# Encoder trunk, head pairs: which of a level half's two side works is issued first

## The chip, the cores and the metric

One NeuronCore of a Trainium2 chip runs the whole program. The metric is the device time of one execution, in microseconds, as the median of several runs.

## The reference

A streaming encoder step with two layers. Each layer mixes tokens through two branches that share one input projection, and then runs an MLP. Tokens are 512 of a prompt and 8 x 16 of running streams, 640 in all; the model width is 1024.

```
z = h @ w_in                                  # one projection for all branches
r, k, v, zw, zi, zg = split(za_mix)           # RWKV-7 branch, 16 heads of 64
S = S * w + (S a) b^T + v k^T ;  y = S r      # per frame, per head
y = group_norm(y) + (sum(r * k * a_rk)) * v ; y = y * gate
# retention branch: 4 heads, chunked; both merged by sigmoid gates, then w_out, then the MLP
```

The kernel computes the recurrence S in blocks of 128 tokens. Inside a block that needs the inverse of a triangular matrix, which is built in levels, each doubling the size of the inverted blocks.

## The kernel before

The 16 heads are worked through in 8 pairs a layer, `rwkv(l, p)`. A pair has five token blocks and two heads, so ten small problems. They are treated in three groups of four, four and two. After products of the blocks (points t, z) come levels 1 to 6. Each level has two halves. In the **T half** TensorE multiplies for each group (marks T), and VectorE multiplies the result by a mask into `T1`. In the **X half** TensorE multiplies T1 (marks X), and ScalarE evicts the result to `XX` or `XTF`. The T half of a level waits for the evictions of the level before it, the X half for the masks. After the levels come a long product (uw) and a chain over the blocks (ca, cb).

Between these dependent pieces the kernel puts independent work of two kinds:

- **Quarters.** While a pair runs, ten tiles of the layer's input projection are made, each in four quarters of 12 matmuls (128x320, with `h_hi`, `h_lo`, `w_hi`, `w_lo`). `point("la3")` issues as many quarters as the table `POINTS` says: two in every half of a level. So a tile starts at each lb and ends at the next la. All tiles use the same two PSUM banks: a tile's first quarter waits until ScalarE has evicted the tile before (L1246, or L1239 for the tiles r, k, v of the next pair). On ScalarE, `point` evicts the tile behind its last quarter, with Copy, Silu or Sigmoid, and then makes the high part `w_hi` of the next weight tile (the high split, L1142). On VectorE, `point` makes its low part `w_lo` (the low split, L1545).
- **Steps of the neighbours.** `side` is a Python generator, one per engine, that first does the group norm of pair p-1 and then prepares pair p+1. `next(side, None)` issues its code up to the next `yield`. All engines call it equally often, so a step stands at the same place on all of them. TensorE's steps, by the name that each marks, lie so: rows behind X1, over behind X2, gate behind X3, wi0 behind T4, wi1 behind X4, ss behind T5, kb behind T6, bs behind X6. The other steps of the levels are empty on TensorE. ss sums squares over channels (128x2 matmuls); ScalarE takes the square root (`KR`, 128x10), VectorE the reciprocal (L1698), and kb spreads it over the channels. wi0 and wi1 feed sigmoids on ScalarE, which then squares k for ss.

Each engine runs its own instructions in the order in which they are written; semaphores (`wait_stage`, `done`) tie the engines together. ScalarE loads a new function table where the next function needs one; the compiler places this instruction. In the levels, pairs 1 and 6 evict a Silu tile in level 4, and pairs 1, 4 and 6 one in level 5; the others evict with Copy there, and pair 7, which prepares nothing, with Sigmoid.

Of the kernel before, what the change touches and what calls it, by code (L numbers as in the profile page):

```python
# [151 lines left out]
def rw_groups(lv):  # L152

    return (0, 1, 2) if lv < S_LEVELS else (0, 1)


def group_blocks(g):

    return range(4 * g, min(4 * g + 4, 2 * NBLK))
# [67 lines left out]
def build(nc, io, outs, scratch):  # L227
# [8 lines left out]
    with ExitStack() as ctx:  # L236
# [388 lines left out]
        def _(pe):  # L625
# [179 lines left out]
            def rwkv(l, p):  # L805
# [3 lines left out]
                point, side = quarters_of(l, f"f{p}"), beside_of(l, p)  # L809
# [42 lines left out]
                for lv in range(1, LEVELS):  # L852
                    for g in rw_groups(lv):
                        if lv == 1:
                            W("ve_in", f"x0.{g}")
                        else:
                            W("ac_in", f"X{lv - 1}.{g}")
                        for m in group_blocks(g):
                            to = slice(64 * (m % 4), 64 * (m % 4) + 64)
                            if lv == LEVELS - 1:  # L860
                                last = mm(ps[64:128, 2 + g, to], LTI[0:64, m, 64:128], XX[0:64, m, 0:64])
                                continue
                            for d in range(2):
                                last = mm(ps[half(d), 2 + g, to], LTI[half(d), m, half(d)], XX[half(d), m, 0:64])
                        M(last, "pe_in", f"T{lv}.{g}")
                    point(f"la{lv}")
                    next(side, None)
                    for g in rw_groups(lv):
                        W("ve_in", f"T{lv}.{g}")
                        for m in group_blocks(g):  # L870
                            at_ = 128 * (m % 4)
                            if lv == LEVELS - 1:
                                last = mm(ps[0:64, 2 + g, 64 * (m % 4):64 * (m % 4) + 64], T1[64:128, m], XTF[64:128, m, 64:128])
                                continue
                            ends = g == 2 and lv == S_LEVELS - 1
                            for d in range(0 if ends else 1 if lv == LEVELS - 2 else 2):
                                mm(ps[half(d), 2 + g, at_:at_ + 64], XX[half(d), m, 64:128], T1[half(d), m])
                            for d in range(2):
                                last = mm(ps[half(d), 2 + g, at_ + 64:at_ + 128], T1[half(d), m], XX[half(d), m, 64:128])
                        M(last, "pe_in", f"X{lv}.{g}")  # L880
                    point(f"lb{lv}")
                    next(side, None)
                W("ac_in", "z")
                W("ac_in", f"X{S_LEVELS - 1}.2")
                for g in (0, 1):
# [237 lines left out]
        def _(ac):  # L1123
# [192 lines left out]
            def rwkv(l, p):  # L1316
                n = PAIRS * l + p
                W = lambda stage, name: wait_stage(ac, stage, n, name)
                M = lambda stage, name: done(stage, n, name)
                point, side = evictions_of(l, f"f{p}"), beside_of(l, p)  # L1320
                for b in range(NBLK):
                    W("pe_tr", f"t{b}")
                    do(TOKB[:, 4 * b:4 * b + 4], ps[:, 6 + b % 2, :].rearrange("p (t n) -> p t n", n=128))
                    M("ac_tr", f"t{b}")
                    point(f"t{b}" if b < PB else "z")
                W("pe_in", "z")
                do(Z_.rearrange("p m n -> p (m n)"), five_blocks(5))
                M("ac_in", "z")
                point("z")
                next(side, None)  # L1330
                point("lt")
                next(side, None)
                for lv in range(1, LEVELS):
                    point(f"la{lv}")
                    next(side, None)
                    for g in rw_groups(lv):
                        W("pe_in", f"X{lv}.{g}")
                        ms = slice(4 * g, 2 * NBLK if g == 2 else 4 * g + 4)
                        k = 2 if g == 2 else 4
                        src = ps[:, 2 + g, 0:128 * k].rearrange("p (t n) -> p t n", n=128)  # L1340
                        if lv == LEVELS - 1:
                            do(XTF[0:64, ms, 64:128], ps[0:64, 2 + g, 0:64 * k].rearrange("p (t n) -> p t n", n=64))
                        elif lv == LEVELS - 2 or g == 2 and lv == S_LEVELS - 1:
                            if g != 2:
                                do(XX[0:64, ms, 0:64], src[0:64, :, 0:64])
                            for d in range(2):
                                do(XTF[half(d), ms, half(d)], src[half(d), :, 64:128])
                        else:
                            do(XX[:, ms], src)
                        M("ac_in", f"X{lv}.{g}")  # L1350
                    point(f"lb{lv}")
                    next(side, None)
                W("pe_in", "uw")
                by_stream = lambda a: a.rearrange("p (m b t) -> p m b t", m=2, t=DEC_T)
                do(WT, ps[:, 4, :].rearrange("p (t n) -> p t n", n=128))
                do(WRS[:, :, :, 0:DEC_T], by_stream(ps[:, 7, 0:128]))
                do(WRS[:, :, :, DEC_T:2 * DEC_T], by_stream(RR[:, p % 2, SEQ:TOK]))
                M("ac_in", "uw")
                point("uw")
                next(side, None)  # L1360
                for c in range(PB):
                    point(f"ca{c}")
                    next(side, None)
                    if c == 0:
                        W("pe_ch", "sT")
                        for e in range(2):
                            do(STS[:, 2 * e:2 * e + 2], ps[:, 5 + e, 0:256].rearrange("p (m e v) -> p m e v", e=2, v=64))
                        M("ac_ch", "sT")
                    if c == 1:
                        W("pe_ch", "su")  # L1370
                        do(SU.rearrange("p (b t) -> p b t", t=DEC_T), ps[:, 6, 0:256].rearrange("p (b n) -> p b n", n=2 * DEC_T)[:, :, 0:DEC_T])
                        M("ac_ch", "su")
                    if c == 3:
                        W("pe_ch", "y")
                        if p:
                            wait_stage(ac, "ve_gn", n - 1, "ya")
                            ac.wait_ge(ya_lo, PAIRS * l + min(p, 4))
                        do(yb[:, 0:SEQ], ps[:, 7, :])
                        do(yb[:, SEQ:TOK].rearrange("p (b t) -> p b t", t=DEC_T), ps[:, 6, 0:256].rearrange("p (b n) -> p b n", n=2 * DEC_T)[:, :, DEC_T:2 * DEC_T])
                        M("ac_ch", "y")  # L1380
                    point(f"cb{c}")
                    next(side, None)
                for _ in side:
                    pass
                W("pe_ch", "spo")
                if n:
                    ac.wait_ge(rw_out, 96 * n)
                do(SPO[0:64, :], ps[0:64, 4, 0:128])
                M("ac_ch", "spo")
                W("pe_ch", "sout")  # L1390
                do(SN, ps[:, 2, :].rearrange("p (b n) -> p b n", n=128))
                M("ac_ch", "sout")
                point("end")
# [129 lines left out]
        def _(ve):  # L1523
# [254 lines left out]
            def rwkv(l, p):  # L1778
# [3 lines left out]
                point, side = low_parts_of(l, f"f{p}"), beside_of(l, p)  # L1782
# [25 lines left out]
                for lv in range(1, LEVELS):  # L1808
                    for g in rw_groups(lv):
                        W("pe_in", f"T{lv}.{g}")  # L1810
                        k = 2 if g == 2 else 4
                        src = ps[:, 2 + g, 0:64 * k].rearrange("p (t n) -> p t n", n=64)
                        if lv == LEVELS - 1:
                            after(ve.tensor_copy(T1[64:128, 4 * g:4 * g + k], src[64:128]))
                        else:
                            c = C_LC + 64 + 64 * lv
                            tt(T1[:, 4 * g:4 * g + k], src, c1[:, None, c:c + 64].to_broadcast([128, k, 64]), MUL_)
                        M("ve_in", f"T{lv}.{g}")
                    point(f"la{lv}")
                    next(side, None)  # L1820
                    point(f"lb{lv}")
                    next(side, None)
                point("uw")
                next(side, None)
                parity = c1[:, None, C_EP:C_EP + 2, None].to_broadcast([128, 2, 2, 64])
# [212 lines left out]
```

## Time and profile before

| | us |
|---|---|
| median of 3 runs | 5024.22 (5024.21 to 5031.55) |
| the profiled execution's own time | 5024.12 |
| its span, first to last instruction | 5022.3 |
| TensorE busy | 4492.5 |
| VectorE busy | 2025.7 |
| ScalarE busy | 1378.9 |

Busy time is that in which an engine executes at least one instruction. A stretch in which one engine is nearly always busy runs at that engine's pace; what others do there costs nothing unless it makes the busy one wait. In a timeline row the numbers are the start and the length in us, and a bracket tells how long the engine stood idle before the row, and for whom. A matmul in f32 appears as two records, so five matmuls read x10. L634 is the helper through which nearly all matmuls go; L1129 is ScalarE's.

### The profile page before, as it was taken

Reading aid. Unit: us, or ns where it says so; the run is one execution under the profiler, and the core shown is the slowest. Engines: PE = TensorE matmul, PEld = TensorE weight load, DVE = VectorE, ACT = ScalarE, POOL = GpSimd, SP = SyncE. Lnnn points to the kernel's source line nnn. Section 1 sums busy time; section 2 is a strip of 40 time slices with the busy share of each in tenths; the row PEclk is TensorE's granted clock in tenths of the full one; section 3 lists DMA queues with packets and bytes.
Section 4 is the critical chain, followed back from the end, with each engine's and each line's share of the span. In section 5 each row is a group of like instructions: output and inputs, shape, how many; then the busy total and the mean of one; then the engine's idle time right before and its main releaser. Section 6 shows DMA issues by size and latency. Waiting matters only on the chain.

```text
span 5022.3 us, 87846 instructions
## 1 busy us (share of the span) xinstructions
PE 4492.5 (89%) x38284; PEld 3916.8 (78%) x38284; DVE 2025.7 (40%) x2870; ACT 1378.9 (27%) x1995; POOL 237.3 (5%) x393
## 2 busy tenths in 40 slices
PE   6899999999987777899978999999999777779997
PEld 1689889888865557899917888888888565569996
DVE  0434444434234444544415444444433444354444
ACT  1333333333211112322303333333332111122222
POOL 0000000000010001000000000000000100100000
PEclk9899999999999988999988999999999999989998
DMA  7211122112343324122261211112124433412221
GB/s 246 65 62 59 59 64 61 60 60 67 127 134 131 132 95 126 44 74 83 61 231 44 64 60 57 60 61 64 59 70 131 156 126 124 128 56 70 71 74 60
DMA packets 481278, 448.78 MB, mean 89 GB/s; under 512 B 17638, under 2 KB 399472, under 8 KB 480000
## 3 DMA queue, kind: packets, MB, share of 16 engines
q1 hardware_dynamic: 432624, 291.02, 18.7%
q0 software_dynamic: 30896, 119.06, 7.2%
q10 hardware_dynamic: 17408, 33.56, 1.7%
q8 instruction: 278, 4.55, 0.4%
q14 instruction: 72, 0.59, 0.0%
HBM read 345.81 MB, written 97.76 MB: 88 GB/s over the span
## 4 chain that ended last, share of the span: by engine, by line
PE 81%; DVE 7%; DMA 7%; ACT 4%; issue 2%; ACTq 0%; DVEq 0%; SPq 0%; POOL 0%; POOLq 0%
PE ps L634 79%; ACT scr L1129 2%; DVE scr L1532 2%; DMA scr<-in_ada_w_dram 2%; PE ps L638 2%; DMA scr<-in_state_ret_dram 2%; DMA out_dram<-scr 1%; DMA w_raw<-in_w_branch_b_dram 1%; DVE scr L1534 1%; ACT w_hi L1142 1%; DVE scr L1610 1%; DVE scr L1919 1%; DVE w_lo L1545 1%; DVE acc L1532 1%; DMA w_raw<-in_w_in_dram 0%
## 5 line engine op out<-in xcount | busy, mean ns | idle before, releaser
L634 PE MATMUL ps<-scr 64*64 64x64 f32 (+10 forms) x15136 | 1164.4, 259 | 133.6 <-DMA scr<-in_state_ret_dram 60.5
L634 PEld LDWEIGHTS ps<-scr 64*64 64x64 f32 (+5 forms) x15136 | 820.8, 146 | 503.2 <-issue 351.5
L634 PE MATMUL ps<-h_hi,w_hi 128*128 128x320 f32 x4288 | 1033.5, 323 | 107.3 <-DVEq L1540 76.8
L634 PE MATMUL ps<-h_lo,w_hi 128*128 128x320 f32 x4288 | 984.5, 311 | 0.0
L634 PE MATMUL ps<-h_hi,w_lo 128*128 128x320 f32 x4288 | 983.0, 311 | 0.0
L634 PEld LDWEIGHTS ps<-h_hi,w_hi 128*128 128x128 f32 x4288 | 707.3, 190 | 161.0 <-issue 126.6
L634 PEld LDWEIGHTS ps<-h_lo,w_hi 128*128 128x128 f32 x4288 | 724.1, 190 | 0.0
L634 PEld LDWEIGHTS ps<-h_hi,w_lo 128*128 128x128 f32 x4288 | 723.9, 190 | 0.0
L1129 ACT ACTIVATE scr<-ps 128x512 f32<-128x512 f32 (+9 forms) x694 | 346.3, 499 | 1344.5 <-PE ps L634 1100.8
L1142 ACT ACTIVATE w_hi<-w_raw 128x1024 fp32r<-128x1024 f32 (+1 forms) x468 | 410.9, 878 | 782.8 <-PE ps L634 681.6
L1545 DVE TENSOR_TENSOR w_lo<-w_raw,w_hi 128x1024 fp32r<-128x1024 f32 (+1 forms) x468 | 469.0, 1002 | 352.6 <-ACT w_hi L1142 339.7
L634 PE MATMUL ps<-r_hi,w_hi 128*128 128x320 f32 x1664 | 391.8, 317 | 137.5 <-DVEq L1540 110.3
L634 PEld LDWEIGHTS ps<-r_hi,w_hi 128*128 128x128 f32 x1664 | 284.6, 193 | 147.4 <-issue 144.6
L634 PE MATMUL ps<-r_lo,w_hi 128*128 128x320 f32 x1664 | 386.9, 314 | 0.0
L634 PE MATMUL ps<-r_hi,w_lo 128*128 128x320 f32 x1664 | 386.2, 314 | 0.0
L1532 DVE TENSOR_TENSOR scr<-ps,c 128x512 f32<-128x512 f32 (+2 forms) x416 | 221.3, 532 | 408.1 <-PE ps L634 372.6
L634 PEld LDWEIGHTS ps<-r_lo,w_hi 128*128 128x128 f32 x1664 | 285.5, 193 | 0.0
L634 PEld LDWEIGHTS ps<-r_hi,w_lo 128*128 128x128 f32 x1664 | 285.2, 192 | 0.0
L1532 DVE TENSOR_TENSOR scr<-scr 128x640 f32<-128x640 f32 (+6 forms) x292 | 263.9, 904 | 15.2 <-ACTq L1228 2.2
L634 PE MATMUL ps<-scr,c 64*64 64x64 f32 (+1 forms) x1024 | 167.4, 316 | 53.7 <-ACTq L1135 51.3
L1534 DVE SCALAR_TENSOR_TENSOR scr<-scr,ps 128x1024 f32<-128x1024 f32 x64 | 78.1, 1221 | 301.9 <-PE ps L634 301.9
L1246 ACT ACTIVATE scr<-ps 128x640 f32<-128x640 f32 x128 | 90.1, 704 | 379.6 <-PE ps L634 379.0
(131 smaller groups left out, 2860.9 us busy)
## 6 DMA issues: line engine op xcount, KB each, us to landing
w_raw<-in_w_in_dram SPq DMA_DIRECT2D x180, 512.0 KB, 3.7
scr<-in_ada_w_dram SPq DMA_DIRECT2D x24, 2048.0 KB, 7.9
scratch_z<-scr SPq DMA_DIRECT2D x128, 320.0 KB, 2.2
scr<-in_state_ret_dram POOLq DMA_DIRECT2D x64, 512.0 KB, 5.3
out_dram<-scr ACTq DMA_DIRECT2D x64, 512.0 KB, 3.4
w_raw<-in_w_ffn_up_dram SPq DMA_DIRECT2D x64, 512.0 KB, 4.0
w_raw<-in_w_ffn_down_dram SPq DMA_DIRECT2D x128, 256.0 KB, 2.8
scr<-scratch_z POOLq DMA_DIRECT2D x8, 2560.0 KB, 9.8
```

Source lines behind the costliest of these rows:

```text
L634: return pe.matmul(out, lhsT, rhs, start=start, stop=stop, skip_group_check=True)
L638: return pe.transpose(out, in_, c1[0:n, C_ID:C_ID + n])
L1129: ac.activation(out, in_, f, **kw).then_inc(ac_order, 1)
L1142: ac.activation(WH[:, s, 0:kt], WR[:, s, 0:kt], ACT.Copy).then_inc(hi_done, 1)
L1246: ac.activation(halves(ZT[:, f % 2]), two_banks(0), fn).then_inc(psum_read_a, 1)
L1532: tt = lambda o, a, b, op: after(ve.tensor_tensor(o, a, b, op))
L1534: stt = lambda o, a, s, b, o0, o1: after(ve.scalar_tensor_tensor(o, a, s, b, o0, o1))
L1545: ve.tensor_tensor(WL[:, s, 0:kt], WR[:, s, 0:kt], WH[:, s, 0:kt].bitcast(F32), SUB).then_inc(lo_done, 1)
L1610: after(ve.reciprocal(RS, RS))
L1919: after(ve.reciprocal(PT[:, 0:TOK], PT[:, 0:TOK]))
```

## The change

In every level half, on TensorE, ScalarE and VectorE, the side step is called ahead of `point` and not behind it. All else stays.

```diff
--- before.py
+++ after.py
@@ -863,8 +863,8 @@
                             for d in range(2):
                                 last = mm(ps[half(d), 2 + g, to], LTI[half(d), m, half(d)], XX[half(d), m, 0:64])
                         M(last, "pe_in", f"T{lv}.{g}")
+                    next(side, None)
                     point(f"la{lv}")
-                    next(side, None)
                     for g in rw_groups(lv):
                         W("ve_in", f"T{lv}.{g}")
                         for m in group_blocks(g):
@@ -878,8 +878,8 @@
                             for d in range(2):
                                 last = mm(ps[half(d), 2 + g, at_ + 64:at_ + 128], T1[half(d), m], XX[half(d), m, 64:128])
                         M(last, "pe_in", f"X{lv}.{g}")
+                    next(side, None)
                     point(f"lb{lv}")
-                    next(side, None)
                 W("ac_in", "z")
                 W("ac_in", f"X{S_LEVELS - 1}.2")
                 for g in (0, 1):
@@ -1331,8 +1331,8 @@
                 point("lt")
                 next(side, None)
                 for lv in range(1, LEVELS):
+                    next(side, None)
                     point(f"la{lv}")
-                    next(side, None)
                     for g in rw_groups(lv):
                         W("pe_in", f"X{lv}.{g}")
                         ms = slice(4 * g, 2 * NBLK if g == 2 else 4 * g + 4)
@@ -1348,8 +1348,8 @@
                         else:
                             do(XX[:, ms], src)
                         M("ac_in", f"X{lv}.{g}")
+                    next(side, None)
                     point(f"lb{lv}")
-                    next(side, None)
                 W("pe_in", "uw")
                 by_stream = lambda a: a.rearrange("p (m b t) -> p m b t", m=2, t=DEC_T)
                 do(WT, ps[:, 4, :].rearrange("p (t n) -> p t n", n=128))
@@ -1816,10 +1816,10 @@
                             c = C_LC + 64 + 64 * lv
                             tt(T1[:, 4 * g:4 * g + k], src, c1[:, None, c:c + 64].to_broadcast([128, k, 64]), MUL_)
                         M("ve_in", f"T{lv}.{g}")
+                    next(side, None)
                     point(f"la{lv}")
                     next(side, None)
                     point(f"lb{lv}")
-                    next(side, None)
                 point("uw")
                 next(side, None)
                 parity = c1[:, None, C_EP:C_EP + 2, None].to_broadcast([128, 2, 2, 64])
```

On TensorE a place in level 5 of pair 0: `scr 64x64 x16` is the T5 product, `c,scr 128x2 x5` the step ss, and `h_..,w_..` are quarters. Before:

```order
L634 MATMUL ps<-h_lo,w_hi 128x320 x2
L634 MATMUL ps<-h_hi,w_lo 128x320 x2
L634 MATMUL ps<-c,scr 128x2 x5
L634 MATMUL ps<-scr 64x64 x24
L634 MATMUL ps<-h_hi,w_hi 128x320 x2
```

and now:

```order
L634 MATMUL ps<-scr 64x64 x16
L634 MATMUL ps<-c,scr 128x2 x5
L634 MATMUL ps<-h_hi,w_hi 128x320 x2
L634 MATMUL ps<-h_lo,w_hi 128x320 x2
L634 MATMUL ps<-h_hi,w_lo 128x320 x2
```

ss stood behind the two quarters and in front of X5; it now stands behind T5 and in front of the quarters.

On ScalarE level 4 of pair 1: L1246 evicts the tile, `r_hi` is the group norm's last step, `ps,par 128x320 x2` are the sigmoids behind wi0 and wi1, `128x4x128 x2` the evictions of X4, `acc,par` the square for ss.

```order
-L1246 ACT_TABLE_LOAD
-L1246 ACTIVATE scr<-ps 128x640
-L1142 ACTIVATE w_hi<-w_raw 128x1024
 L1129 ACTIVATE r_hi<-scr 128x640
 L1129 ACT_TABLE_LOAD
 L1129 ACTIVATE scr<-ps,par 128x320 x2
-L1129 ACTIVATE scr<-ps 128x4x128 x2
+L1246 ACT_TABLE_LOAD
+L1246 ACTIVATE scr<-ps 128x640
+L1142 ACTIVATE w_hi<-w_raw 128x1024
+L1129 ACTIVATE scr<-ps 128x4x128 x2
+L1129 ACT_TABLE_LOAD
```

The tile's eviction and the high split went behind the step, and one table load more stands between the two pairs of sigmoids.

On VectorE from the reciprocal of level 5 to the multiply behind kb in level 6 of pair 0 (`w_lo` is a low split, L1814 the mask step of T6, `scr<-scr,ps` the multiply):

```order
 L1698 RECIPROCAL scr<-scr 128x10
+L1545 TENSOR_TENSOR w_lo<-w_raw,w_hi 128x1024
 L1814 COPY scr<-ps 64x256 x2
 L1533 TENSOR_SCALAR scr<-scr,par 128x640
 L1534 SCALAR_TENSOR_TENSOR acc<-scr,acc 128x640
 L1534 SCALAR_TENSOR_TENSOR scr<-acc,par 128x640
-L1545 TENSOR_TENSOR w_lo<-w_raw,w_hi 128x1024
 L1532 TENSOR_TENSOR scr<-scr,ps 128x640
```

The low splits moved behind the step: one from ahead of the reciprocal to behind it, one from ahead of the multiply to behind it.

## Rows read from the trace of the kernel before

**Rows 1.** The page: the span and its first part, busy time by engine.

```profile
span 5022.3 us, 87846 instructions
...
PE 4492.5 (89%) x38284; PEld 3916.8 (78%) x38284; DVE 2025.7 (40%) x2870; ACT 1378.9 (27%) x1995; POOL 237.3 (5%) x393
```

**Rows 2.** Busy time (instructions) in two stretches: pairs of layer 0, of layer 1.

```profile
260.00:1320.00 1060.00, 1046.80 (x12137) 941.60 (x12137) 432.27 (x759) 357.14 (x566) 42.42 (x70) 1.00 0.20 62
2750.00:3830.00 1080.00, 1066.44 (x12311) 959.72 (x12311) 438.81 (x767) 363.33 (x577) 46.05 (x76) 1.00 0.20 63
```

**Rows 3.** The chain of waits of TensorE, stretch 260 to 1320.

```profile
PE ps L634 <- ACT scr L1246: 9.3, 12, 1.7
PE ps L634 <- ACTq L1228: 3.9, 7, 1.6
```

**Rows 4.** Timeline of TensorE (start, us), pair 1 of layer 0, levels 4 to 6.

```profile
437.78 0.56 PE L634 MATMUL ps<-h_hi,w_hi 128*128 128x320 f32 x2
...
441.50 0.81 PE L634 MATMUL ps<-scr,lw 64*128 64x320 f32 x4
442.24 2.08 PE L634 MATMUL ps<-scr 64*64 64x64 f32 x64
...
448.70 1.22 PE L634 MATMUL ps<-scr 64*64 64x64 f32 x32
449.85 0.56 PE L634 MATMUL ps<-h_hi,w_hi 128*128 128x320 f32 x2
...
453.47 1.17 PE L634 MATMUL ps<-c,scr 128*128 128x2 f32 x10
454.57 2.08 PE L634 MATMUL ps<-scr 64*64 64x64 f32 x48
456.58 0.56 PE L634 MATMUL ps<-h_hi,w_hi 128*128 128x320 f32 x2
...
460.29 1.14 PE L634 MATMUL ps<-scr 64*64 64x64 f32 x16
461.36 0.55 PE L634 MATMUL ps<-h_hi,w_hi 128*128 128x320 f32 x2
...
465.07 1.31 PE L634 MATMUL ps<-c,scr 128*64 128x128 f32 x20
```

**Rows 5.** Timeline of ScalarE in the same pair and levels.

```profile
441.65 1.28 ACT L1246 ACT_TABLE_LOAD   x1 [8.33 <-PE ps L634]
...
447.82 1.31 ACT L1129 ACTIVATE scr<-ps 128x512 f32<-128x512 f32 x2
449.26 1.09 ACT L1129 ACTIVATE scr<-ps,par 128x320 f32<-128x320 f32 x2
450.74 0.83 ACT L1129 ACTIVATE scr<-acc,par 128x640 f32<-128x640 f32 x1 [0.40 <-DVEq L1663]
453.72 1.28 ACT L1246 ACT_TABLE_LOAD   x1 [2.15 <-PE ps L634]
455.01 0.70 ACT L1246 ACTIVATE scr<-ps 128x640 f32<-128x640 f32 x1
...
456.56 2.51 ACT L1129 ACTIVATE scr<-ps 64x256 f32<-64x256 f32 x6
...
460.47 0.18 ACT L1129 ACTIVATE scr<-ps 128x10 f32<-128x10 f32 x1
```

**Rows 6.** Timeline of VectorE in the same pair, levels 5 and 6.

```profile
460.80 0.17 DVE L1533 TENSOR_SCALAR scr<-scr 128x10 f32<-128x10 f32 x1 [1.22 <-ACTq L1228]
461.01 0.22 DVE L1698 RECIPROCAL scr<-scr 128x10 f32<-128x10 f32 x1
...
463.97 0.89 DVE L1534 SCALAR_TENSOR_TENSOR scr<-acc,par 128x640 f32<-128x640 f32 x1
```

**Rows 7.** Timeline of TensorE behind the last pair, where a step precedes quarters.

```profile
1338.05 1.17 PE L634 MATMUL ps<-c,scr 128*128 128x2 f32 x10
1339.08 0.54 PE L634 MATMUL ps<-h_hi,w_hi 128*128 128x320 f32 x2
```

## Prediction, written before the changed kernel ran

> **What bounds the kernel now.** I read the page first: TensorE (PE) is busy for 4492.5 of 5022.3 us, the next engine, VectorE, for 2025.7 [rows 1]. The change touches only the stage of the head pairs, so I asked for the busy time of that stage in both layers. There PE is busy for 1046.80 of 1060.00 us and for 1066.44 of 1080.00 us, at the full granted clock of 1.00, which is 2.4 GHz [rows 2]: 13.2 and 13.6 us of idle time are all that better cover could win. The chain of waits says what they are in layer 0: 9.3 us in 12 waits for a tile's eviction (L1246) and 3.9 us in 7 waits at a pair's start [rows 3]. By their place in the timeline these lie at the points uw, ca and cb and at the pair's first transposes; none lies in a level, which is where the change is. So the stage goes at the pace of PE's own instructions, and an edit matters if it makes PE wait or changes what it costs to go from one kind of matmul to the next.
>
> **What moves.** In each of six levels a T half and an X half both had: products of the level, two quarters (24 matmuls), the side step. Now the step stands ahead of the quarters. Nothing is added on PE, VectorE, SyncE or GpSimd. DMA issues keep their order; SyncE's loads wait for the low splits, which VectorE now does up to one step later. On ScalarE two table loads a layer are added, in pairs 1 and 6, where the tile evicted in level 4 is a Silu tile and now comes between two uses of Sigmoid.
>
> A pair's active PE steps in the levels are rows, over, gate (pairs 1 to 7) and wi0, wi1, ss, kb, bs (pairs 0 to 6): 3 x 14 + 5 x 14 = 112 moved steps. Each used to have two quarters, 3.71 us (456.58 to 460.29 in [rows 4]), in front of it as cover for what it waits for. That cover now stands behind it. For each I ask what its input's chain takes.
>
> **Terms that come to nothing.** rows needs a VectorE and a ScalarE instruction behind the T masks, over a small sqrt with its table load, gate one multiply: each chain is under 4 us, against the T half's quarters and the X products (3.71 + 2.01 us) that still lie between. wi0 and wi1 wait for work a half level older. bs waits for kb's multiply on VectorE: from the reciprocal at 461.01 to the end of three more operations (463.97 + 0.89) takes 3.9 us [rows 6]; with a low split (about 1.1) now in between and the multiply (0.8) behind, some 6.0 us, against 0.4 + 1.24 + 3.71 + 1.07 = 6.4 us until PE is at bs. It fits by 0.4 us. The low splits that come later feed a tile that starts a level (11 us) on.
>
> **The term kb (level 6).** kb waits for the reciprocal of the root of ss. That chain runs over ScalarE, which serves in this order: eviction of level 5's tile, high split, six evictions of X5, table load, sqrt; then VectorE's max and reciprocal. Its start is tied to the end of the T5 quarters, and these now come later, since ss is ahead of them. Count from the end of T5, E. PE: ss to quarters 1.03 (1338.05 to 1339.08 in [rows 7]), quarters to X5 3.71, X5 2.01 (454.57 to 456.58), quarters 3.71, T6 1.07 (460.29 to 461.36) [rows 4]: PE is at kb at E + 11.53. The chain: the eviction starts 3.87 us behind its quarters' start (449.85 to 453.72), and the reciprocal ends 6.22 us behind the eviction (455.01 to 461.23) [rows 4 to 6]; a release takes 0.15 us (460.65 to 460.80). Ready at E + 1.03 + 3.87 + 6.22 + 0.15 = E + 11.27. It fits, by 0.26 us.
>
> Where the level-5 tile is Silu, a table load stands ahead of its eviction (453.72 to 455.01, 1.29 us): ready at E + 12.56, and PE **waits 1.03 us**. Before, it hid: kb came only at 465.07. These are pairs 1, 4 and 6: 3 x 1.03 = 3.1 us a layer. X5's quarters then also wait some 0.3 us for that eviction, but within the same 1.03.
>
> **The term ss (level 5), pairs 1 and 6.** With both table loads of level 4: wi0 at 437.78, its quarters at 438.52 (wi0 0.74), load at +3.87 = 442.39, eviction 443.68, behind it and the split (1.55) X4's evictions 445.23, 1.44 us on the added load 446.67, the two sigmoids 447.96, the square 449.16, done 449.99, released 450.14 [rows 4, 5]. PE is at ss at 438.52 + 3.71 + 2.01 + 0.74 + 3.71 + 1.07 = 449.76. It **waits 0.4 us**: 0.8 a layer.
>
> A load costs 1.28 us and the next activation starts 0.01 us later [rows 5]. The Trainium skill (ScalarE: Activation LUTs, What ACT_TABLE_LOAD costs) adds a drain of about 1.38 us to each switch. By that rule the wait at ss would be 1.8 us, and the sum 5.5 us higher; by the row, 0.4.
>
> **Borders between kinds of matmul.** For ss: before, T5 to quarters 1.07, quarters to ss 3.62 (449.85 to 453.47), ss to X5 1.10 (453.47 to 454.57), in all 5.79. Now T5 to ss, which no row shows (I take 1.07 to 1.15), 1.03 and 3.71: 5.81 to 5.89. I take +0.05 for each of 28 such steps (rows and ss), 1.4 us, and zero for the others, whose parts (0.74, 3.71) are the same on either side. Bounds from the nearest rows: 0.1 us either way for 112 steps, 11 us.
>
> **Sum.** 2 x (3.1 + 0.8) + 1.4 = 9.2 us on the profiled execution's own 5024.12 us, 5033.3; the median of the runs shown, 5024.22, is 0.1 above that one. **I predict 5033 us.** About 0.2%, 10 us, is what a measurement can tell from no change, so this stands at the border.
>
> **Rivals.**
> A, all hidden: 5024 to 5028. If the ScalarE chain gets shorter than I add up, or borders give back 0.05 us a step (-5.6 us). For it: work that has nothing to do moves ahead; against it, the chain of 6.22 us has no idle gap to lose. 0.20.
> B, the plain pairs wait too. The margin of 0.26 us in pairs 0, 2, 3, 5 is within what a few semaphores take; 0.3 us more in the chain costs all 14 steps 0.3: 4 us, 5037. 0.18.
> C, a border costs more: the step's first load behind 64x64 products takes 0.1 to 0.2 us longer than the quarters' did. 112 steps: 11 to 22 us, 5044 to 5055. It decides from 0.1 us on. The Trainium skill (TensorEngine Tiling (Array Packing), Key Properties) states that a change of tiling mode drains TensorE; but the changes of mode are here as many as before, only between other neighbours. 0.08.
> D, a table switch costs 2.66 us at ss, as the page has it: 5038 to 5039. The rows speak against it. 0.05.
> E, faster: early steps let ScalarE and VectorE run ahead, so that the waits of 13.2 + 13.6 us at uw, ca, cb shrink. More than 19 of these 27 must go for it to show against my 9 us: 5007 to 5014. Against it: these waits are for an eviction just behind its own quarters, which move with them. 0.04.
> My own case, 5029 to 5037, has 0.45.
>
> **Numbers.** Within 0.2% (to 5034.2): two thirds or more of my case (0.32), A (0.20) and a little of B (0.03), 0.55. Slower: the rest of mine 0.13, of B 0.15, C 0.08, D 0.05, 0.41. Faster 0.04. Of both signs little is left for the one below; the range 5026 to 5041 leaves out C, E and the low end of A.
>
> **What would show it.** Right: new waits of PE of about 1 us ahead of kb in pairs 1, 4, 6 alone, for VectorE's reciprocal, and 0.4 us ahead of ss in 1 and 6; ScalarE with four more table loads; ss to kb 11.5 us in plain pairs. Wrong: waits at kb in every pair (B), none (A), more time between the same instructions with no wait named (C), fewer waits at ca and uw (E). It fails most easily by the margins of 0.26 and 0.4 us, which are sums of five durations.

## The result, and the profile after

The changed kernel takes 5034.51 us (median of 20 runs, 5028.68 to 5040.04), the kernel before 5024.22 us over 20 runs. The ratio is 1.002, with a 95% interval of 1.0013 to 1.0027: slower by 10.3 us, or 6.5 to 13.6 us by the interval. Forecast were 5033 us and a range of 5026 to 5041; the time lies right at the border between "no change" and "slower" that the prediction drew, and a little beyond it.

The page, first the span and busy time by engine, as in [rows 1]:

```profile
span 5038.2 us, 87850 instructions
PE 4508.3 (89%) x38284; PEld 3925.9 (78%) x38284; DVE 2027.1 (40%) x2870; ACT 1379.0 (27%) x1999; POOL 237.4 (5%) x393
```

PE executes the same 38284 matmuls; ScalarE has 1999 instructions and not 1995, the four added table loads. PE's busy time rose by 15.8 us, most of it outside the changed part (see the last section).

The waits of PE in the stretch of layer 0's pairs (260 to 1325 us), as in [rows 3] (releaser, then us in total, times, longest):

```profile
PE ps L634 <- ACT scr L1246: 10.0, 15, 1.7
PE ps L634 <- ACTq L1228: 4.6, 9, 1.6
PE ps L634 <- DVEq L1663: 1.9, 3, 0.6
```

Three kinds came: three waits for VectorE (L1663 is its semaphore increment in the steps), two more for ScalarE's steps, three more for evictions. Where they are, the timeline of PE shows; pair 1 of layer 0, to be held against [rows 4] (start, length, then idle before the row):

```profile
447.72 1.15 PE L634 MATMUL ps<-scr 64*64 64x64 f32 x32
449.08 1.28 PE L634 MATMUL ps<-c,scr 128*128 128x2 f32 x10 [0.22 <-ACTq L1228]
450.22 0.54 PE L634 MATMUL ps<-h_hi,w_hi 128*128 128x320 f32 x2
...
453.91 2.08 PE L634 MATMUL ps<-scr 64*64 64x64 f32 x48
456.21 0.53 PE L634 MATMUL ps<-h_hi,w_hi 128*128 128x320 f32 x2 [0.22 <-ACT scr L1246]
...
459.89 1.14 PE L634 MATMUL ps<-scr 64*64 64x64 f32 x16
461.67 1.31 PE L634 MATMUL ps<-c,scr 128*64 128x128 f32 x20 [0.64 <-DVEq L1663]
```

ss waits 0.22 us, the quarters behind X5 wait 0.22, kb waits 0.64. ScalarE and VectorE in the same pair, against [rows 5, 6]:

```profile
454.07 1.28 ACT L1246 ACT_TABLE_LOAD   x1 [5.08 <-PE ps L634]
455.36 0.70 ACT L1246 ACTIVATE scr<-ps 128x640 f32<-128x640 f32 x1
455.96 1.05 ACT L1142 ACTIVATE w_hi<-w_raw 128x1024 fp32r<-128x1024 f32 x1
456.91 2.50 ACT L1129 ACTIVATE scr<-ps 64x256 f32<-64x256 f32 x6
459.51 1.28 ACT L1129 ACT_TABLE_LOAD   x1
460.80 0.18 ACT L1129 ACTIVATE scr<-ps 128x10 f32<-128x10 f32 x1
```

```profile
461.14 0.17 DVE L1533 TENSOR_SCALAR scr<-scr 128x10 f32<-128x10 f32 x1 [4.91 <-ACTq L1228]
461.35 0.22 DVE L1698 RECIPROCAL scr<-scr 128x10 f32<-128x10 f32 x1
```

The chain from the load to the reciprocal's end is 454.07 to 461.57, 7.50 us, and it has no gap over 0.2 us: it is as long as before (453.72 to 461.23, 7.51). What moved are its start and PE. Counted from the end of T5 in a plain pair, one without a Silu tile (pair 2 of layer 0), PE is at kb after 11.62 us (585.78 to 597.40) where it took 15.22 (585.35 to 600.57), and the quarters that start the chain begin 1.14 us later.

**Level time** is what the rest of this text compares: from the first of a pair's lt products to its first uw product, read from the starts in PE's timeline. It holds all six levels and nothing else. In the table it is given for the pairs of layer 1, where no stretch at half clock fell into a pair's levels, save with ScalarE's old order (see there and at the end); layer 0 agrees within 0.07 us a pair but for such stretches.

| level time, us, layer 1 | pair 0 | 1 | 2 | 3 | 4 | 5 | 6 | 7 | more than before, both layers |
|---|---|---|---|---|---|---|---|---|---|
| before | 71.31 | 75.88 | 75.81 | 75.82 | 75.82 | 75.82 | 75.81 | 71.01 | |
| changed | 71.42 | 77.31 | 76.04 | 76.04 | 77.09 | 76.09 | 77.67 | 71.12 | 11.0 |
| ss back | 71.31 | 75.93 | 75.94 | 75.94 | 76.01 | 75.94 | 76.01 | 71.12 | 1.9 |
| kb back | 71.42 | 77.14 | 76.04 | 76.04 | 76.85 | 76.04 | 77.44 | 71.12 | 9.6 |
| kb alone | 71.31 | 75.88 | 75.82 | 75.82 | 76.98 | 75.82 | 76.97 | 71.01 | 4.8 |
| kb and bs | 71.31 | 75.90 | 75.83 | 75.83 | 75.90 | 75.83 | 75.90 | 71.01 | 0.5 |
| levels 1 to 3 alone | 71.31 | 75.98 | 75.92 | 75.93 | 75.92 | 75.92 | 75.92 | 71.12 | 1.4 |
| ScalarE's old order | 75.23 | 84.07 | 81.80 | 81.81 | 84.10 | 79.61 | 83.44 | 72.45 | 90 |
| no Silu, old order | 71.30 | 75.81 | 75.81 | 75.82 | 75.81 | 75.82 | 75.81 | 71.01 | |
| no Silu, new order | 71.43 | 76.04 | 76.04 | 76.04 | 76.04 | 76.08 | 76.05 | 71.12 | 3.2 (than the row above) |

The last column sums the differences over 16 pairs, less 1.5 us where a stretch at half clock fell into pair 6 of layer 0 (changed, kb back). The changed kernel's 11.0 us accounts for the whole measured loss of 10.3 us, within its interval of 6.5 to 13.6.

### The profile page after: what moved, and what is told of

The parts are those of the page before. It is cut to its first block, busy times and chain, and to the rows that moved or that the text cites. A ratio compares the mean times of both kernels' runs of the same rounds, so it can differ in the third digit from the quotient of the medians.

```text
span 5038.2 us, 87850 instructions
## 1 busy us (share of the span) xinstructions
PE 4508.3 (89%) x38284; PEld 3925.9 (78%) x38284; DVE 2027.1 (40%) x2870; ACT 1379.0 (27%) x1999; POOL 237.4 (5%) x393
## 4 chain that ended last, share of the span: by engine, by line
PE 80%; DVE 7%; DMA 6%; ACT 4%; issue 2%; ACTq 0%; DVEq 0%; SPq 0%; POOL 0%; POOLq 0%
PE ps L634 78%; ACT scr L1129 3%; DVE scr L1532 2%; DMA scr<-in_ada_w_dram 2%; PE ps L638 2%; DMA scr<-in_state_ret_dram 2%; DMA out_dram<-scr 1%; DMA w_raw<-in_w_branch_b_dram 1%; DVE scr L1534 1%; ACT w_hi L1142 1%; DVE scr L1610 1%; DVE scr L1919 1%; DVE w_lo L1545 1%; DVE acc L1532 1%; ACT scr L1246 0%
## 5 line engine op out<-in xcount | busy, mean ns | idle before, releaser
L634 PE MATMUL ps<-scr 64*64 64x64 f32 (+10 forms) x15136 | 1165.6, 259 | 129.2 <-DMA scr<-in_state_ret_dram 57.1
L634 PEld LDWEIGHTS ps<-scr 64*64 64x64 f32 (+5 forms) x15136 | 822.1, 146 | 490.6 <-issue 349.4
L634 PE MATMUL ps<-h_hi,w_hi 128*128 128x320 f32 x4288 | 1034.5, 323 | 108.7 <-DVEq L1540 77.1
L634 PE MATMUL ps<-h_lo,w_hi 128*128 128x320 f32 x4288 | 982.7, 311 | 0.0
L634 PE MATMUL ps<-h_hi,w_lo 128*128 128x320 f32 x4288 | 981.6, 310 | 0.0
L634 PEld LDWEIGHTS ps<-h_hi,w_hi 128*128 128x128 f32 x4288 | 708.2, 189 | 177.3 <-issue 147.3
L634 PEld LDWEIGHTS ps<-h_lo,w_hi 128*128 128x128 f32 x4288 | 722.6, 189 | 0.0
L634 PEld LDWEIGHTS ps<-h_hi,w_lo 128*128 128x128 f32 x4288 | 722.2, 189 | 0.0
L1129 ACT ACTIVATE scr<-ps 128x512 f32<-128x512 f32 (+9 forms) x694 | 345.0, 497 | 1320.5 <-PE ps L634 1082.6
L634 PE MATMUL ps<-r_hi,w_hi 128*128 128x320 f32 x1664 | 393.2, 318 | 134.8 <-DVEq L1540 110.3
L634 PEld LDWEIGHTS ps<-r_hi,w_hi 128*128 128x128 f32 x1664 | 285.5, 194 | 144.8 <-issue 142.0
L634 PE MATMUL ps<-r_lo,w_hi 128*128 128x320 f32 x1664 | 387.7, 315 | 0.0
L634 PE MATMUL ps<-r_hi,w_lo 128*128 128x320 f32 x1664 | 387.0, 314 | 0.0
L634 PEld LDWEIGHTS ps<-r_lo,w_hi 128*128 128x128 f32 x1664 | 286.8, 193 | 0.0
L634 PEld LDWEIGHTS ps<-r_hi,w_lo 128*128 128x128 f32 x1664 | 285.9, 193 | 0.0
L634 PE MATMUL ps<-scr,c 64*64 64x64 f32 (+1 forms) x1024 | 177.1, 330 | 50.8 <-ACTq L1135 50.4
L1129 ACT ACTIVATE scr<-scr 128x640 f32<-128x640 f32 (+6 forms) x182 | 119.6, 657 | 316.3 <-DVEq L1663 195.8
```

Of the source, the lines that this page charges most:

```text
L634: return pe.matmul(out, lhsT, rhs, start=start, stop=stop, skip_group_check=True)
L1129: ac.activation(out, in_, f, **kw).then_inc(ac_order, 1)
```

## The experiments

The first edits use a helper in place of the two lines, so that each level half of each engine can be chosen. It moves the lines of the kernel: L634, L1129, L1246, L1228 and L1663 are L647, L1140, L1257, L1239 and L1672 there.

```diff
+def half_of(eng, name, point, side):
+    if name in STEP_FIRST[eng]:
+        next(side, None)
+        point(name)
+    else:
+        point(name)
+        next(side, None)
```

**1. ss back.** `STEP_FIRST` holds all halves but la5.

> As the changed kernel, but in the T half of level 5 (the step ss) the quarters stand ahead of the step again, on all three engines. Level time below is the time from the lt products to the product uw in the trace of a pair (before: 75.82 us in pairs 2 to 5). Theory (chain tied to the T5 quarters): with ss behind them these quarters start 1.03 us earlier, so the reciprocal is ready at E + 11.53 us and TensorE is at kb at E + 11.51: no wait above 0.1 us is left at kb or ss, pairs 1, 4 and 6 take as long as the plain ones, each about 0.2 us above before, and the kernel takes 5027 us. Rival 1 (kb's own loss of cover is enough): the waits of 0.64 us at kb stay in pairs 1, 4, 6 and the time is about 5032. Rival 2 (the cost is in the borders): one step of eight less, 5033 to 5034.

Measured: 5026.27 us (11 runs), ratio to before 1.0001 (0.9991 to 1.001). In layer 0's pairs PE's waits are those of the kernel before, row by row:

```profile
PE ps L647 <- ACT scr L1257: 9.3, 12, 1.7
PE ps L647 <- ACTq L1239: 3.9, 7, 1.6
```

Every new wait is gone, with kb's quarters still behind it. So it was not enough that kb lost its cover: the chain that feeds it had to start late as well. In pair 1 the chain is again 7.50 us long (453.85 to 461.35) and ends 0.14 us ahead of kb at 461.49. Where PE waits for the reciprocal, kb starts 0.1 us behind its end (461.57 to 461.67 in the changed kernel), so less than 0.05 us is to spare, as the first theory had it. 0.12 us of borders a plain pair is left.

**2. kb back.** All halves but la6.

> As the changed kernel, but in the T half of level 6 (the step kb) the quarters stand ahead of the step again. Theory: kb has its 3.7 us of cover again and never waits; what is left are the waits of 0.2 to 0.5 us at ss in pairs 1 and 6 and the wait of 0.2 us for the eviction of level 5 in pairs 1, 4 and 6, so pair 4's level time is 0.4 us above before, pair 1's 0.6, pair 6's 0.9, the plain ones' 0.2: 5029 us. Rival 1 (ss's place is what costs, kb only shows it): hardly a gain on the changed kernel, 5033. Rival 2 (borders): 5033 to 5034.

Measured: 5032.3 us (11 runs), ratio 1.0005 (0.9996 to 1.0014), level times 9.6 us above before. This is a miss: pairs 4, 1 and 6 are 1.03, 1.26 and 1.63 us above before, not 0.4, 0.6 and 0.9, and of 1.43 us in pair 1 only 0.17 went. The level times decide here, since the interval of the totals holds both no change and most of the loss. Rival 1 had forecast this (hardly a gain), but not the place of the wait. kb does not wait, but bs does, a step further on (PE, pair 1):

```profile
464.85 1.31 PE L647 MATMUL ps<-c,scr 128*64 128x128 f32 x20
466.09 1.14 PE L647 MATMUL ps<-scr 64*64 64x64 f32 x16
467.70 1.34 PE L647 MATMUL ps<-scr,c 128*128 128x320 f32 x4 [0.47 <-DVEq L1672]
```

and VectorE at that place:

```profile
461.52 0.22 DVE L1707 RECIPROCAL scr<-scr 128x10 f32<-128x10 f32 x1
461.88 1.23 DVE L1554 TENSOR_TENSOR w_lo<-w_raw,w_hi 128x1024 fp32r<-128x1024 f32 x1
463.14 1.00 DVE L1823 COPY scr<-ps 64x256 f32<-64x256 f32 x2
464.29 0.56 DVE L1542 TENSOR_SCALAR scr<-scr,par 128x640 f32<-128x640 f32 x1
464.88 0.83 DVE L1543 SCALAR_TENSOR_TENSOR acc<-scr,acc 128x640 f32<-128x640 f32 x1
465.74 0.89 DVE L1543 SCALAR_TENSOR_TENSOR scr<-acc,par 128x640 f32<-128x640 f32 x1
466.77 0.82 DVE L1541 TENSOR_TENSOR scr<-scr,ps 128x640 f32<-128x640 f32 x1
```

From the reciprocal's end at 461.74 VectorE works without a gap over 0.2 us until it can release bs at 467.70, 5.96 us. This is the chain that the prediction had put at 6.0 us and found to fit by 0.4 us. In the changed kernel's pairs 1, 4 and 6 it fits because PE has just waited at kb. Take that wait away, and it comes back at bs.

**3. kb alone.** `STEP_FIRST` is {la6}.

> As the kernel before, with only the T half of level 6 (the step kb) changed. Theory: the quarters of T5 still start 1.03 us earlier than in the changed kernel, so kb's input is ready at E + 11.53 us in the pairs with a Silu tile, against E + 11.51 for TensorE: a wait of 0 to 0.1 us, level times within 0.15 us of before, 5024 us. Rival (kb alone loses its cover): waits of about 1 us at kb in pairs 1, 4 and 6, 5030 us.

Measured: a single run, 5030.29 us. No wait at kb, as the theory had it, though by as little as in experiment 1 (the reciprocal ends 0.14 us ahead of kb in pairs 1, 4 and 6), and pairs 1, 2, 3, 5 are as before. But pairs 4 and 6 take 1.2 us more, which neither theory foresaw. PE in pair 4 of layer 0:

```profile
875.84 1.14 PE L647 MATMUL ps<-scr 64*64 64x64 f32 x16
878.14 0.53 PE L647 MATMUL ps<-h_hi,w_hi 128*128 128x320 f32 x2 [1.16 <-ACT scr L1257]
```

ScalarE:

```profile
876.00 1.28 ACT L1257 ACT_TABLE_LOAD   x1 [5.83 <-PE ps L647]
877.29 0.70 ACT L1257 ACTIVATE scr<-ps 128x640 f32<-128x640 f32 x1
```

All tiles use one pair of PSUM banks. In pairs 4 and 6 the level-6 tile is Silu, so its eviction needs 2.0 us behind the load's start. Before, kb and X6 lay between the tile's last quarter and the next tile's first; with kb moved ahead X6's 1.07 us are left, and PE waits for the bank. The step was cover for the eviction. The explanation was put to the test:

**4. kb and bs.** `STEP_FIRST` is {la6, lb6}.

> As the kernel before, with both halves of level 6 changed (steps kb and bs). In the run with kb alone, pairs 4 and 6 waited 1.16 us for the eviction of the level-6 tile, which is Silu there: TensorE had only X6 (1.07 us) between the tile's last quarter and the next tile's first. Theory: bs, moved ahead of that first quarter, gives 0.9 to 1.1 us back, so the wait is at most 0.3 us and the level times of pairs 4 and 6 fall from 77.0 to 76.1 us. Rival (the wait is for something else that kb's move delays, for instance ScalarE's order): it stays at 1.1 us.

Measured: a single run, 5026.68 us; pairs 4 and 6 at 75.90 us, 0.08 above before and 1.1 below the run with kb alone. Shown for level 6: what the la half loses as cover for the bank, the lb half gives back by its own step.

**5. ScalarE's old order.** PE and VectorE as in the changed kernel, `STEP_FIRST["ac"]` empty.

> As the changed kernel, but ScalarE keeps its old order (a tile's eviction and high split ahead of the step) in all level halves. Theory (a step is only as early as the engine that feeds it): wi1 on TensorE now comes at 5.7 us behind the start of the T4 quarters, while ScalarE gets to wi0's sigmoids behind eviction, split, in pairs 1 to 4 the group norm's conversion, and the table load, ready at 7.9 to 8.8 us, 1.3 later with a Silu tile: waits at wi1 of 2.2 us in pairs 0 and 5, 3.1 in 2 to 4, 4.4 in 1, 3.5 in 6; over waits 1.1 us in pairs 1 to 7. In all about 60 us, 5086. Rival (the idle ScalarE has slack everywhere): no more than the changed kernel, 5034.

Measured: 5116.75 us (4 runs), ratio 1.0176 (1.016 to 1.0191). The waits in layer 0's pairs:

```profile
PE ps L647 <- ACTq L1239: 24.9, 14, 4.2
PE ps L647 <- ACT scr L1257: 10.0, 15, 1.7
PE ps L647 <- DVEq L1672: 9.9, 10, 1.2
```

At wi1 they are 2.24 us in pairs 0 and 5, 2.94 in 2 to 4, 4.22 in 1 and 3.52 in 6, at over 1.13 to 1.20: the sizes expected, within 0.2 us, and 58 us in all. The engine that feeds a step has to serve it as early as PE wants it. The sum was too low by a third (60 us against 90). Most of the rest is clock: 12 stretches at half clock fell into the levels, two of them twice as long as the others, and at 1.5 us for each of the short ones (see the end) that is some 21 us, an estimate. Waits at kb and at X5's quarters, which I had left out, are 5 us, the borders 3. In the windows view around pair 1's wait at wi1 (columns: stretch, length, PE, PEld, VectorE, ScalarE and GpSimd busy, granted clock, DMA share, GB/s):

```profile
444.20:454.10 9.90, 5.86 (x90) 5.47 (x88) 2.07 (x5) 5.80 (x7) 0.00 (x0) 1.00 0.12 43
454.20:457.60 3.40, 3.31 (x11) 2.45 (x12) 2.83 (x4) 2.59 (x5) 0.00 (x0) 0.50 0.00 0
457.60:467.00 9.40, 9.40 (x106) 8.95 (x106) 5.36 (x14) 1.19 (x2) 0.00 (x0) 1.00 0.21 58
```

PE was busy for 5.86 of 9.90 us, and then the granted clock was 0.50 (1.2 GHz) for 3.4 us.

**6 and 7. No Silu.** The kernel before and the changed one with the Silu of the retention gate left out (Copy is used):

```diff
-                            fn = ACT.Sigmoid if o >= Z_ALL else ACT.Silu if o % 12 >= 8 else ACT.Copy
+                            fn = ACT.Sigmoid if o >= Z_ALL else ACT.Copy
```

> The kernel before with Copy in place of Silu where the spilled gate tiles are evicted (the silu of the retention gate is left out of the computation), so that no table load stands ahead of these evictions. It is the base for the next one. Both theories: level times as before, 75.8 us in pairs 1 to 6, since nothing waits in the levels with or without the loads; total 5018 to 5024 (the 1.3 us longer waits at uw and ca behind Silu tiles fall away, about 4 us).

> The changed kernel with the same Copy in place of Silu (the silu of the retention gate is left out). Theory: without the table load no step waits; the level time of every pair 1 to 6 is that of the run with the old order plus 0.22 us, all of it borders between kinds of matmul, and in all it is 3.1 us slower than that run. Rival (the waits come from VectorE's later low split or from a smaller margin than summed): waits of 0.3 to 1 us at kb stay, 6 to 11 us slower.

Measured, a single run each: 5009.19 and 5021.94 us. Level times differ by 0.22 to 0.26 us in pairs 1 to 6, 3.2 us in all, and PE's waits in layer 0's pairs are the same in both:

```profile
PE ps L647 <- ACT scr L1257: 5.8, 9, 1.7
PE ps L647 <- ACTq L1239: 2.6, 7, 0.4
```

So every new wait needs the table load of a Silu tile, and the rest is borders. The two totals are 12.8 us apart, against 3.2 in the levels. With one execution each this is not the order's doing: of the rest 1.5 us are a stretch at half clock behind pair 6 of layer 0, and 8.1 us lie outside the pairs, which the order does not touch; single runs of one kernel differ as much. The first total is 9 us under the range expected. The pairs of the two layers are 12.9 us shorter than before, not 4: PE's waits outside the levels fell by some 4.8 us a layer (in layer 0 from 13.2 to 8.4), and the two stretches at half clock, 1.5 us each, did not occur among the pairs of this execution.

**8. Levels 1 to 3 alone** (rows, over, gate).

> As the kernel before, with only levels 1 to 3 changed (the steps rows, over, gate of the group norm). Theory: no new wait, no table load more; three borders of 0.03 us a pair: level times of pairs 1 to 7 up by 0.1 us, 5025 to 5026 us. Rival (each early step costs by itself, 11 us over 112 steps): 0.3 us a pair, 5028 us.

Measured: a single run, 5021.9 us; no new wait, 0.10 us a pair, 1.4 us in all, as the first theory had it. The total is under the 5025 to 5026 us expected, by less than single runs of the kernel before differ.

**9 and 10. One quarter less at uw.** The waits that both kernels have lie behind uw, so I tried to move the changes of tile there, from each kernel:

```diff
-POINTS = {"t": 1, "z": 1, "lt": 0, "la": 2, "lb": 2, "uw": 2, "ca": 1, "cb": 1, "pre": 1, "post": 2, "end": 99}
+POINTS = {"t": 1, "z": 1, "lt": 0, "la": 2, "lb": 2, "uw": 1, "ca": 1, "cb": 1, "pre": 1, "post": 2, "end": 99}
```

> The kernel before with one quarter instead of two at the point uw, so that all quarters behind it come one point later and the tenth tile's last one comes at the pair's end. Tiles then change at cb0 and cb2, with 1.2 to 1.6 us of products between an eviction's start and the next tile, not 0.5. Theory: the waits of 0.46 to 1.74 us at ca0 and of 0.79 us at ca2 and that of 0.37 us at the pair's start, 13.2 us a layer, fall to 2 to 6 us: 5004 to 5014 us. Rival (the cover that uw loses was needed): TensorE waits behind uw for ScalarE's three instructions, which end 1.4 us behind uw, or at the pair's end for the last tile's eviction: no gain, 5022 to 5030.

> The changed kernel with one quarter instead of two at uw. Theory: both effects add, since they lie in different parts of a pair: level times as in the changed kernel (5.5 us a layer above before), the waits at ca and uw as in the run with the old order: 5014 to 5024 us. Rival (the two share a cover): more than 3 us away from that sum.

Measured: 5030.62 us (11 runs), ratio to before 1.0008 (0.9999 to 1.0017), and 5041.53 us (7 runs), 1.003 (1.0019 to 1.0042). Both are misses, with no gain in the totals. With the old order layer 0's pairs show:

```profile
PE ps L634 <- ACT scr L1246: 11.6, 17, 1.7
```

The waits at a pair's start (3.9 us) went, but there are 17 waits for evictions now in place of 12: 0.39 us or 1.66 at the first change of tile and 0.46 at the second. 13.2 us became 11.6. I had taken the products between two tiles for longer than they are. The traces do show a small gain in the pairs: from pair 0's first lt product to pair 7's first uw product the two layers take 1022.0 and 1021.3 us, against 1023.6 and 1023.1 before, with equally many stretches at half clock. It is too small for the totals. Level times are those of the kernels without this edit, save the 1.5 us of a stretch at half clock and 0.2 us in pair 6 of layer 0, so the two edits hardly touch each other; the two totals are 10.9 us apart.

## Why the prediction was right

The mechanism was right: which steps wait, in which pairs, and for what. One term of the sum was too small by more than half, the borders. That 5033 lies so near is no finer proof: the interval of 6.5 to 13.6 us holds the forecast of 9.2 and the 11.0 of the level times alike.

**Bound.** Right: the stage goes at PE's pace, and nothing was won, since no wait lay in a level. E did not happen.

**kb, 1.03 us in pairs 1, 4, 6.** Right in place, cause and size: in layer 0 the trace has 0.22 us at X5's quarters and 0.64 at kb, in layer 1 0.18 and 0.68, parts of one chain as argued; pair 4's levels take 1.27 us more, and without the 0.22 of borders that a plain pair shows this is 1.05. That it needs both the late start of the T5 quarters and the table load is shown by experiments 1, 3 and 7.

**ss, 0.4 us in pairs 1 and 6.** 0.22 in pair 1 and 0.51 to 0.52 in pair 6, in both layers. The cause is right; that the average fits the 0.4 is in part luck. The chain had been worked out for pair 1, where T5 takes 1.14 us and not 1.07 and ss starts 0.09 us behind the square's end and not 0.15. Pair 6 has a hold of 0.4 us on ScalarE between two of its instructions with no other engine as releaser; it appears at two different places in the two layers. What it is stays open. The added load took 1.28 us, and the next activation started 1.30 us behind its start (445.65 to 446.95), so D did not happen. The Trainium skill (ScalarE: Activation LUTs, What ACT_TABLE_LOAD costs) has 2.66 us for each switch; a wait of 1.8 us at ss is the estimate from that figure. The measurement decides.

**bs fits by 0.4 us.** It fits, but by less: in pair 1 the multiply ends 0.28 us ahead of bs (467.42 to 467.70), of which a release takes 0.11 (467.59 to 467.70 in experiment 2). The prediction's sum had left the release out. In pairs 1, 4 and 6 it fits only because PE waits at kb (experiment 2).

**Plain pairs fit by 0.26 us.** Right: no wait in pairs 0, 2, 3, 5 in either layer. In pair 2 of layer 0 the reciprocal ends 0.42 us ahead of kb (596.98 to 597.40); less a release of 0.11 this is 0.31. B did not happen.

**Borders, 1.4 us.** The term that was mis-sized: 3.2 us (experiments 6 and 7). Here is ss in a plain pair (pair 2 of layer 0), from the end of T5 to the start of X5, first before, then changed:

```profile
585.35 0.56 PE L634 MATMUL ps<-h_hi,w_hi 128*128 128x320 f32 x2
...
588.97 1.17 PE L634 MATMUL ps<-c,scr 128*128 128x2 f32 x10
590.07 2.08 PE L634 MATMUL ps<-scr 64*64 64x64 f32 x48
```

```profile
585.78 1.28 PE L634 MATMUL ps<-c,scr 128*128 128x2 f32 x10
586.92 0.54 PE L634 MATMUL ps<-h_hi,w_hi 128*128 128x320 f32 x2
...
590.61 2.07 PE L634 MATMUL ps<-scr 64*64 64x64 f32 x48
```

Before, the quarters took 3.62 us and ss 1.10, now ss takes 1.14 and the quarters 3.69: 0.11 us more, where the prediction took 0.05. It had read ss at 1.03 us from a place where quarters stand on both sides of it [rows 7]; directly behind 64x64 products it takes 0.11 more. The quarters give little of that back: behind ss they are 0.02 us shorter than behind 64x64 products (3.69 against 3.71). rows shows the same four durations, and 28 such steps make 3.1 us. The other steps are within 0.01 us of their old cost, gate and bs included. The experiments agree: three steps of levels 1 to 3 cost 0.10 together (experiment 8), leaving ss out saves 0.10 (experiment 1), and kb and bs cost 0.01 together (experiment 4). The prediction's "T5 to quarters 1.07" is 1.15 in its own rows (448.70 to 449.85) and 1.08 in this plain pair; it stands on both sides of the comparison and changes little. C, a tenth of a microsecond for every step, did not happen.

**Sum.** Forecast were 7.8 of waits and 1.4 of borders. Measured are 11.0 in the levels, of which 3.2 are borders, so that 7.8 are left for the waits. PE's idle time named in the traces is 6.6 us in 16 waits; the other 1.2 would be 0.07 us a wait, about the overlap of a product's end with the next one's start (T6 runs 1.14 us, and the next product starts 1.07 us behind its start), which a wait ends.

**What I had not seen.** That a step ahead of the quarters no longer covers the eviction, beyond the one place at X5 where the prediction had it (0.3 us, measured 0.22). In the change all halves move together, so it costs nothing else; moved alone, kb costs 2.4 us a layer (experiment 3).

## What to carry to other kernels

Where one engine is always busy and two kinds of filler share its gaps, the order of the two decides which waits are covered: count for each wait the work between the release of its input and its use, on all engines, and expect a removed wait to come back at the next use along the chain. A margin that fits by a few tenths of a microsecond in most rounds fails in those with an extra table load, so look for the rounds that differ. And move a step only together with the engine that feeds it: the same edit without ScalarE's part cost 90 us instead of 10.

## What the runs showed of the hardware

In the kernel before the granted clock fell to 1.2 GHz behind a wait of 1.74 us in pair 2 of layer 0, and not behind the same wait in the changed one. The two kernels' windows over the same instructions, first before, then changed:

```profile
620.70:636.60 15.90, 15.08 (x148) 12.86 (x149) 6.89 (x15) 7.72 (x12) 0.00 (x0) 0.89 0.17 56
```

```profile
621.30:635.70 14.40, 13.60 (x149) 11.53 (x149) 6.90 (x15) 7.72 (x12) 0.00 (x0) 1.00 0.19 61
```

The same work took 15.90 and 14.40 us. Each of the two executions has two such stretches among its pairs: the kernel before behind waits of 1.74 and 1.70 us in pair 2 of either layer, the changed one behind the wait of 0.51 us at ss in pair 6 of layer 0 and behind one of 1.74 us later in that pair. The first of these makes the pair's level time 79.24 us where layer 1 has 77.67. Which of the waits is followed by a lower clock differs between executions, and each time costs 1.5 us.

The profiled executions are 15.9 us apart, 11.0 of it from pair 0's first lt product to pair 7's first uw product of the two layers. The larger part of the rest lies behind the last pair of layer 1, in code that is the same in both kernels: 1243.3 us and then 1250.0, with PE busy for 1042.4 and 1054.3 us at a mean granted clock of 0.94 and 0.93. That is also most of the 15.8 us by which PE's busy time rose. Single totals of the kernel before spread over 16 us (5015.23 to 5031.55), more than the change is worth; so the level times, not the totals, carry the comparison here.
